# Building the S5 Toeplitz matrices from padded strips: full rows, one issuing queue, no zeroing

## The reference

```python
bu = jnp.einsum('blgn,gpn->blgp', uf.astype(jnp.complex64), b_bar)
a = jnp.broadcast_to(lam_bar, (1, seq, S5_GROUPS, S5_STATE))
_, states = lax.associative_scan(_linear_recurrence_combine, (a, bu), axis=1)
y = jnp.einsum('gnp,blgp->blgn', c, states).real + d.astype(f32) * uf
y = jax.nn.gelu(y.reshape(bsz, seq, D_MODEL))
y = y * jax.nn.sigmoid(y @ glu_w.astype(f32) + glu_b.astype(f32))
```

## Time and profile before

| | us |
|---|---|
| median of 3 runs | 1308.99 (1308.8 to 1311.32) |
| the profiled execution, its own time | 1309.56 |
| its span, first to last instruction | 1307.8 |
| PE busy | 1253.6 (96%) |
| DVE busy | 694.8 (53%) |
| ACT busy | 465.5 (36%) |
| POOL busy | 58.1 (4%) |

### The profile page before, as it was taken

One profiled execution on the slowest core, in us unless ns is written; L12 is line 12 of the kernel. 1 busy time (PEld: TensorE's weight loads), 2 busy tenths in 40 slices (PEclk: granted clock), 3 DMA queues, 4 the chain that ended last, 5 costly groups with the idle time before them and its releaser, 6 DMA issues.

```text
span 1307.8 us, 16043 instructions
## 1 busy us (share of the span) xinstructions
PE 1253.6 (96%) x6253; PEld 1039.9 (80%) x6253; DVE 694.8 (53%) x822; ACT 465.5 (36%) x481; POOL 58.1 (4%) x64
## 2 busy tenths in 40 slices
PE   2779999999999999999999999999999999999997
PEld 2768778888887888888888888888788888887886
DVE  8797874444444445555556464554355454444433
ACT  4834544242423333324223332332233232323222
POOL 2960000000000000000000000000000000000000
PEclk9989999999999999999999999999999999999999
DMA  5053323333322323322313223233332323222231
GB/s 112 2 136 100 96 88 105 96 96 96 96 86 81 96 88 114 103 100 96 105 33 121 79 65 103 65 96 96 97 97 88 104 90 102 90 72 89 88 101 73
DMA packets 147791, 119.18 MB, mean 91 GB/s; under 512 B 12857, under 2 KB 140017, under 8 KB 147761
## 3 DMA queue, kind: packets, MB, share of 16 engines
q1 hardware_dynamic: 143584, 115.78, 28.5%
q10 hardware_dynamic: 4176, 2.98, 1.1%
HBM read 114.29 MB, written 2.10 MB: 89 GB/s over the span
## 4 chain that ended last, share of the span: by engine, by line
PE 89%; DVE 4%; ACT 3%; issue 1%; DMA 1%; ACTq 1%; SPq 0%; DVEq 0%
PE bank L673 25%; PE bank L675 25%; PE bank L674 25%; PE bank L769 2%; PE bank L770 2%; PE bank L771 2%; PE bank L780 1%; ACTq L398 1%; DVE w_lo L1126 1%; PE bank L797 1%; PE bank L795 1%; PE bank L796 1%; DVE tmp L1116 1%; DMA w_raw<-in_s_glu_w_dram 1%; PE bank L625 1%
## 5 line engine op out<-in xcount | busy, mean ns | idle before, releaser
L673 PE MATMUL bank<-u_hi,w_hi 128*128 128x512 f32 x960 | 375.5, 391 | 2.0 <-DVE xT L1390 1.1
L675 PE MATMUL bank<-u_hi,w_lo 128*128 128x512 f32 x960 | 374.0, 390 | 0.0
L674 PE MATMUL bank<-u_lo,w_hi 128*128 128x512 f32 x960 | 373.8, 389 | 0.0
L1126 DVE TENSOR_TENSOR w_lo<-w_raw,w_hi 128x2048 fp32r<-128x2048 f32 x112 | 256.7, 2292 | 200.2 <-ACT w_hi L850 199.8
L850 ACT ACTIVATE w_hi<-w_raw 128x2048 fp32r<-128x2048 f32 x112 | 213.5, 1906 | 188.6 <-PE bank L675 146.4
L673 PEld LDWEIGHTS bank<-u_hi,w_hi 128*128 128x128 f32 x960 | 180.3, 188 | 40.5 <-issue 2.0
L675 PEld LDWEIGHTS bank<-u_hi,w_lo 128*128 128x128 f32 x960 | 180.3, 188 | 37.6
L674 PEld LDWEIGHTS bank<-u_lo,w_hi 128*128 128x128 f32 x960 | 180.3, 188 | 37.4 <-issue 0.5
L673 PE MATMUL bank<-h_hi,w_hi 128*128 128x512 f32 x352 | 137.3, 390 | 2.8 <-DVE w_lo L1126 2.8
L674 PE MATMUL bank<-h_lo,w_hi 128*128 128x512 f32 x352 | 137.1, 389 | 0.0
L675 PE MATMUL bank<-h_hi,w_lo 128*128 128x512 f32 x352 | 137.0, 389 | 0.0
(11 more groups left out here) (199 smaller groups left out, 1352.2 us busy)
## 6 DMA issues: line engine op xcount, KB each, us to landing
w_raw<-in_ret_w_qkvg_dram SPq DMA_DIRECT2D x24, 1024.0 KB, 5.0
w_raw<-in_ffn_w_gate_dram SPq DMA_DIRECT2D x22, 1024.0 KB, 5.1
w_raw<-in_ffn_w_up_dram SPq DMA_DIRECT2D x22, 1024.0 KB, 5.1
w_raw<-in_ffn_w_down_dram SPq DMA_DIRECT2D x32, 704.0 KB, 4.2
w_raw<-in_ret_w_o_dram SPq DMA_DIRECT2D x8, 1024.0 KB, 5.1
w_raw<-in_s_glu_w_dram SPq DMA_DIRECT2D x4, 1024.0 KB, 6.0
s<-in_x_dram ACTq DMA_DIRECT2D x2, 1024.0 KB, 12.2
s_w<-in_x_dram SPq DMA_DIRECT2D x1, 2048.0 KB, 10.0
```

The lines of the kernel that those rows point to most:

```text
L673: pe.matmul(o, w_hi[w][:, w_cols], hi, start=first, stop=False)
L674: pe.matmul(o, w_hi[w][:, w_cols], lo, start=False, stop=False)
L675: return pe.matmul(o, w_lo[w][:, w_cols], hi, start=False, stop=end)
L1126: dve.tensor_tensor(w_lo[s][:, :], w_raw[:, s, :], w_hi[s][:, :].bitcast(F32), ALU.subtract).then_inc(w_lo_ready[s], 1)
```

## The change

Each strip now carries its own zeros. Four pairs j lie interleaved (element m of pair i at 4 m + i), behind `LEAD` = 448 zeros, so that a row of four matrices shifted by 16 r columns is one run of 512 floats that starts 64 r floats earlier. One DMA moves, for one r, one half and eight pairs, 16 full rows of 2 x 512 floats (64 KB), zeros included; `toep` is no longer zeroed by ACT. Instead POOL zeroes the leading parts of the strips once at the start (64 partitions x 1792). `toeplitz(queue, part)` issues the 16 DMAs of a part, and SP issues all four parts: part 0 ahead of the x load, parts 1 and 2 behind it, part 3 behind the first GLU load. `strip_out` writes with a stride of four floats, and `y_inputs` reads `toep` with that stride. Strip 1 moves up between the tables of the last input stage (c = 3), strip 4 ahead of the transposes of x; `y_inputs` 0 to 3 no longer wait for `seg_done` 2 (0 and 1 wait for their part only, 2 and 3 for `seg_done` 1), strip 6 comes ahead of that wait and `keep_clock` behind it. ACT issues no Toeplitz DMA any more; it runs a small Gelu right behind strip 6 and splits the first GLU weights between gelu 3 and 4 instead of ahead of gelu 0.

```diff
     if _c == 2:
-        S5_FILLS += [("strip", 0)]
+    if _c >= 2:
+        S5_FILLS += [("strip", _c - 2)]
...
-S5_FILLS += [("b", 6), ("b", 7), ("strip", 1), ("strip", 7), ("strip", 2), ("strip", 3)]
+S5_FILLS += [("b", 6), ("b", 7), ("strip", 2), ("strip", 7), ("strip", 3)]
+Y_BANK = [6, 7, 2, 3, 0, 1, 4, 5]
...
-    _place(_fill, SHARED + _n % 4)
+    _place(_fill, SHARED + _n % 2)
 for _kind in ("y", "yt"):
     for _k in range(8):
-        _place((_kind, _k), _k)
+        _place((_kind, _k), Y_BANK[_k])
...
+LEAD = (STEPS - 1) * N * JB
+GROUP = LEAD + P * JB
...
-        toep = r_1[:, :].rearrange("p (g m) -> p g m", g=G)
+        toep = r_1[:, :].rearrange("p (h k m) -> p h k m", h=2, k=NBLK)
-        strip = w_raw[0:2 * N, :, :].rearrange("p s a -> p (s a)").rearrange("p (j m) -> p j m", j=J)
+        strip = w_raw[0:4 * N, :, 0:2 * GROUP].rearrange("p s (k m) -> p s k m", k=2)
...
-        def toeplitz_half(queue, part, half):
-            queue.wait_ge(toep_zeroed, 2 * part + 2)
+        def toeplitz(queue, part):
             for k in (2 * part, 2 * part + 1):
                 b, fill = S5_AT[("strip", k)]
                 queue.wait_ge(bank_free[b], fill + 1)
-            js = slice(PART * part, PART * part + PART)
-            gs = slice(J * half + js.start, J * half + js.stop)
-            for r in range(STEPS):
-                queue.dma_start(toep[N * r:N * r + N, gs, N * r:P],
-                                strip[N * half:N * half + N, js, 0:P - N * r]).then_inc(toep_loaded[part], 16)
+            for half in range(2):
+                row = 2 * N * (part // 2) + N * half
+                for r in range(STEPS):
+                    at = LEAD - N * JB * r
+                    queue.dma_start(toep[N * r:N * r + N, half, 2 * part:2 * part + 2, :],
+                                    strip[row:row + N, part % 2, :, at:at + P * JB]).then_inc(toep_loaded[part], 16)
...
+            sp.wait_ge(pads_zeroed, 1)
+            toeplitz(sp, 0)
             b, fill = S5_AT[("tb", 4 * NTAB - 1)]
             sp.wait_ge(bank_full[b], fill + 1)
             sp.wait_ge(tb_ready, 2 * NTAB)
             sp.wait_ge(tc_last_ready, 1)
             sp.dma_start(x_tok, x[0].rearrange("(t p) d -> p t d", p=P)).then_inc(x_loaded, 16)
-            toeplitz_half(sp, 0, 0)
-            toeplitz_half(sp, 0, 1)
-            toeplitz_half(sp, 1, 0)
-            toeplitz_half(sp, 2, 0)
-            for part in range(2):
+            toeplitz(sp, 1)
+            toeplitz(sp, 2)
+            for part in (0, 2):
                 sp.wait_ge(toep_loaded[part], 16 * 2 * STEPS)
             load_unit(0, 0, glu_v[:, :, 0:256], KT, 256)
-            toeplitz_half(sp, 3, 0)
-            for part in range(2, 4):
+            toeplitz(sp, 3)
+            for part in (1, 3):
...
-            strips(1)
+            strips(2)
             strips(NBLK - 1)
-            strips(2)
             strips(3)
+            strips(4)
...
-            strips(4)
             strips(5)
...
-                    pe.matmul(o, u[:, jj, half, :], toep[:, J * half + jj, :], start=(jj % 4 == 0), stop=False)
+                    pe.matmul(o, u[:, jj, half, :], toep[:, half, jj // JB, jj % JB::JB],
+                              start=(jj % 4 == 0), stop=False)
+            pe.wait_ge(toep_loaded[0], 16 * 2 * STEPS)
+            y_inputs(0)
+            y_inputs(1)
+            pe.wait_ge(seg_done, 1)
+            pe.wait_ge(toep_loaded[1], 16 * 2 * STEPS)
+            y_inputs(2)
+            y_inputs(3)
+            strips(6)
             pe.wait_ge(seg_done, 2)
-            for k in range(4):
-                if k % 2 == 0:
-                    pe.wait_ge(toep_loaded[k // 2], 16 * 2 * STEPS)
-                y_inputs(k)
-            strips(6)
+            keep_clock(s5_open("y", 6)[0], 8)
             pe.wait_ge(toep_loaded[2], 16 * 2 * STEPS)
             y_inputs(4)
             y_inputs(5)
-            keep_clock(s5_open("y", 6)[0], 8)
             for k in range(4):
                 y_states(k)
             pe.wait_ge(toep_loaded[3], 16 * 2 * STEPS)
...
-            toeplitz_half(act, 1, 1)
...
-            toeplitz_half(act, 2, 1)
             strip_out(6)
-            split_weights(0, 0)
-            toeplitz_half(act, 3, 1)
+            act.activation(small[:, 25:26], eps[:, :], ACT.Gelu_apprx_tanh)
...
                 gelu(k)
+                if k == 3:
+                    split_weights(0, 0)
...
             pool.memset(fb[:, :, :, :], 0.0).then_inc(fb_zeroed, 1)
+            pool.memset(strip[:, :, :, 0:LEAD], 0.0).then_inc(pads_zeroed, 1)
```

More of the change, by code:

```diff
@@ L332, in trunk @@
         tc_ready = sem("tc_ready")
-        toep_zeroed = sem("toep_zeroed")
+        pads_zeroed = sem("pads_zeroed")
         diag_ready = sem("diag_ready")
@@ L575, in strips @@
                 ps, full = s5_open("strip", k)
+                o = ps[2 * N * (k // 4):2 * N * (k // 4) + 2 * N, :]
                 for i in range(JB):
                     for ri in range(2):
[L578 removed]
+                        pe.matmul(o[:, P * i:P * i + P], fb[:, ri, JB * k + i, :],
                                   r_tc[:, ri, JB * k + i, :, :], start=(i == 0 and ri == 0), stop=False)
                 for i in range(JB):
[L581 removed]
+                    mm = pe.matmul(o[:, P * i:P * i + N], ident[0:2 * N, 0:2 * N], d_diag[:, JB * k + i, :],
                                    start=False, stop=(i == JB - 1))
@@ L594, in _ @@
                     pe.wait_ge(diag_ready, 1)
-                    strips(0)
+                if c >= 2:
+                    strips(c - 2)
                 s5_tables(c, 1)
@@ L903, in s5_input_out @@
                      ps[:, :].rearrange("p (j r c) -> p j r c", j=JB, r=2)).then_inc(free, 1)
-            def zero_toeplitz(k):
-                g = PART * (k // 2) + J * (k % 2)
-                act.activation(toep[:, g:g + PART, :].rearrange("p g m -> p (g m)"),
-                               eps[:, :].broadcast_to([P, 8 * P]), ACT.Copy, scale=0.0).then_inc(toep_zeroed, 1)
             def s5_steps_out(k):
@@ L916, in strip_out @@
                 ps, free = s5_full("strip", k)
-                copy(strip[:, JB * k:JB * k + JB, :].rearrange("p j m -> p (j m)"), ps[0:2 * N, :]).then_inc(free, 1)
+                rows32 = slice(2 * N * (k // 4), 2 * N * (k // 4) + 2 * N)
+                copy(strip[rows32, k % 4 // 2, k % 2, LEAD:GROUP].rearrange("p (m i) -> p i m", i=JB),
+                     ps[rows32, :].rearrange("p (i m) -> p i m", i=JB)).then_inc(free, 1)
             s5_table_out(0, 0)
@@ L925, in _ @@
                 s5_input_out(2 * c - 2)
-                if c == 2:
-                    strip_out(0)
-                if c == NTAB - 1:
-                    zero_toeplitz(2)
+                if c >= 2:
+                    strip_out(c - 2)
                 s5_table_out(c, 1)
                 s5_input_out(2 * c - 1)
-                if c < NTAB - 1:
-                    zero_toeplitz(c - 1)
-                else:
-                    act.wait_ge(tb_ready, 2 * NTAB)
-                    for ri in range(2):
-                        copy(ct_last[:, ri, :, :], ct[:, ri, J - JB:J, :]).then_inc(ct_copied, 1)
+            act.wait_ge(tb_ready, 2 * NTAB)
+            for ri in range(2):
+                copy(ct_last[:, ri, :, :], ct[:, ri, J - JB:J, :]).then_inc(ct_copied, 1)
             s5_input_out(NBLK - 2)
             s5_input_out(NBLK - 1)
-            strip_out(1)
-            zero_toeplitz(3)
+            strip_out(2)
             strip_out(7)
-            for k in range(4, 8):
-                zero_toeplitz(k)
-            strip_out(2)
             strip_out(3)
-            toeplitz_half(act, 1, 1)
+            strip_out(4)
             for k in range(KT):
@@ L950, in _ @@
                 copy(xT[:, k, :], ps[:, :]).then_inc(free, 1)
-            strip_out(4)
             strip_out(5)
-            toeplitz_half(act, 2, 1)
             strip_out(6)
-            split_weights(0, 0)
-            toeplitz_half(act, 3, 1)
+            act.activation(small[:, 25:26], eps[:, :], ACT.Gelu_apprx_tanh)
             def gelu(k):
```

1 line of the change is left out of this document (removed).

## The result

| | before | after |
|---|---|---|
| median of the runs beside each other, us | 1309.35 (1308.8 to 1311.32) | 1320.21 (1319.99 to 1320.78) |
| ratio, 95% interval | | 1.0079, 1.0065 to 1.0092 |
| the profiled execution, its own time | 1309.56 | 1320.78 |
| its span | 1307.8 | 1318.9 |

A forecast was written before the change was run, and what follows sets the result against it. It took part 3 of toep, landed at 110.1, as the bound; SP's single line would bring it at 114.4, 4.3 us later, rounded to 3.6: 1309.56 + 3.6 = 1313.2 profiled, median 1312.6, range 1304 to 1316.5.

The forecast's parts named there:

- the fast rival: SP's queue: long runs issue like DRAM loads, at 0.46 us; part 3 lands 4.0 us earlier, 1305.0; chance 0.2.
- Steps 1 and 2: Strip 1 on PE ends at 58.25, its strided copy takes 0.6 (bounds 0.6 and 1.1); SP starts part 0 at 58.95.
- Step 3: SP's queue: part 0 takes 9.9 us, to 68.9; x, issued then, lands 10.0 later, at 78.9.
- Step 5: Strip 5 on PE takes 2.2, to 87.6, and is out of PSUM at 88.3, 1.3 us earlier than before.
- Step 7: SP's queue: GLU load 0.6, part 3 9.9 plus 0.7 for a stretched issue, to 111.6; landing 2.8 later, 114.4.
- a rival of 8%: PE's y_inputs: the 16 B strided read halves the pace, 2.0 us more, 1314.6; chance 0.08.
- The other banks of y only let `y_inputs` 0 to 3 start early; nothing: PE's y products: new banks allow an earlier start only in a stretch that isn't the bound; cost nothing.
- The clock: Rival: PE idles 4.5 us for part 3, its clock falls for 7 us, 3.5 more, 1316; chance 0.1.
- The rounding from 4.3 down to 3.6: Part 3's delay on PE's path, cut because errors of steps 2 to 5 were thought to lean lower.

The follow-up runs named there:

- e9: Kernel before with strips 4 to 6 and keep_clock moved ahead, SP issuing all of part 1, ACT its halves of parts 2 and 3 back to back: 1309.73 us, ratio 1.0004.
- e12: e9 unchanged, run again for ten more runs and a second profile, against the kernel before: 1309.71 us, ratio 1.0.
- e4: Changed kernel plus 14 idle products behind y_states 3, ahead of the wait for part 3, to keep the clock: 1320.65 us, ratio 1.0084 to the kernel before.
- e5: Changed kernel with the x load issued ahead of part 0 on SP, as before the change: 1320.51 us, ratio 1.0076 to the kernel before.
- e1: Changed kernel with ACT again issuing the second halves of parts 1 to 3 (two queues): 1318.45 us, ratio 1.007 to the kernel before.
- e7: As e1, but each DMA moves only the columns right of its shift (output not the reference's): 1316.57 us, ratio 1.0046 to the kernel before.
- e8: Changed kernel with two issuing queues, unit stride and y in banks 0 to 7 in order, together: 1311.93 us, ratio 1.0018 to the kernel before.
- e14: e8 with SP issuing the first GLU load behind its half of part 3, not ahead: 1309.43 us, ratio 1.0 to the kernel before.
- e3: Changed kernel with y in banks 0 to 7 in order and y_inputs 0 to 3 again behind seg_done 2: 1319.23 us, ratio 1.0078 to the kernel before.
- e2: Changed kernel without interleaving: each matrix has its own 112 zeros, strip_out and y_inputs at unit stride: 1319.68 us, ratio 1.0079 to the kernel before.
- e10: Kernel before with each Toeplitz DMA moving full, unshifted rows of 64 KB (output not the reference's): 1316.26 us, ratio 1.0049.
- e13: e9 with SP issuing the first GLU load only when part 2 has landed: 1306.99 us, ratio 0.998 to the kernel before.
- e11: e9 with 14 idle products added ahead of strip 6 to keep the clock: 1313.8 us, ratio 1.0025 to the kernel before.

## Why the prediction was right in sign and wrong in size

**What held.** The GLU's start is what moves, and it comes out one for one at the end. The bound is the arrival of part 3 through SP's line. The issue of a full row costs what a short one did: 0.635 from start to start against the 0.62 taken; the fast rival (0.46) is dead. Part 2 took 12.3 us from its first issue to its landing against 12.1, the transposes of x 6.46 against 6.5. PE waited 3.56 us for part 3, where 4.5 was forecast; that these are close is luck, since part 3 came 3.3 us later than forecast and `y_states` 3 ended 4.3 later (114.16, not 109.9).

**The steps that failed**, in the order of the sum:

- *Steps 1 and 2, +1.7.* SP starts on part 0 at 60.66, not 58.95. 0.5 is `strip_out`, which with its 16-byte stride takes the upper bound, 1.11, not the lower that was chosen. The other 1.2 lie in the stretch before; it differs by 1.0 between two executions of one kernel as well (x issued at 66.78 in e9, at 65.80 in e12), so no cause in the change is shown for it.
- *Step 3, +1.4 and -1.3.* Part 0 has an issue of 1.42 us; x lands 8.7 us after its issue, not 10.0 (why was not tried). They cancel.
- *Step 5, +0.5.* The copy of strip 5 takes 1.08, again the stride.
- *Step 7, +2.0 and -1.1.* Two issues of 1.83 us instead of one small stretch of 0.7: part 3 was done issuing at 116.0, not 111.6. It landed 1.7 us later, not 2.8: the load had been through at 109.48, ahead of the last issues.
- *`y_inputs` at a stride, taken as 0: +1.9.* The bound of +1.97 was the right end. It was called a rival of 8% and kept out of the sum on the ground that a strided stationary load costs PE nothing; but that is the other operand, and no row spoke of the moving one.
- *"The other banks of y only let `y_inputs` 0 to 3 start early; nothing": +1.1.* Looked at for what it releases early, not for who opens banks 0 and 1 next. That is the GLU, at the end of the stretch.
- *The clock: +0.5.* The rival was right that it falls (PE idle 3.56), but it put 3.5 us on it. Only the transposes lost; the strided `y_inputs` take 3.83 at full clock (e4) and 3.90 at half (e5).
- *The rounding from 4.3 down to 3.6: -0.7*, in the wrong direction. The errors leaned the other way, because each unknown had been taken near its low end.

Sum: 3.6 forecast, and 1.7 + 0.1 + 0.5 + 0.2 (part 2) + 0.9 + 1.9 + 1.1 + 0.5 + 0.7 = 7.6 from these points, 11.2 in all by these rounded terms; measured 11.05 at the GLU's start. The range was too narrow for two reasons. Costs with the same sign were each put at their low end and their high ends never added: part 3 at 114.4 + 0.5 + 0.5 (the two copies) is 5.3 us late, and with 1.9 for the stride that is 7.2, or 1316.2, already at the end of the range (1316.5) without any stretched issue beyond the 0.7. The 3.9 us beyond that were put at nothing or not foreseen: 1.2 in the stretch ahead of strip 1, 1.1 for the banks, 0.9 for the stretched issues of part 3 less its quicker landing, 0.5 for the clock, 0.2 for part 2.

**What the experiments add.** The cause is not one thing. The line of issues sets the time in the changed kernel (e5, where an earlier x wins nothing). Behind it, level with each other, lie the transfers of part 3 and PE's own chain with the stride (e1: 115.57 and 115.4); e7 takes the first away and is held by the second. With both eased (e8), the load ahead of part 3 is what is left (e14). The wait for banks stands by itself at the end (e3). The Trainium skill (SBUF — State Buffer, Door 1: The DMA port swizzle) says that an access which crosses into another 16-byte line pays; what e2 measures agrees, for both engines, at a stride of exactly 16 B: 7.46 against 3.71 us for 64 records on PE, 1.11 against 0.59 for a copy on ACT. The Trainium skill's rule to coalesce small transfers (DMA: Bandwidth & Descriptors, Rules for kernel authors) gets no support from filling rows up to 64 KB: the issue gets no cheaper (0.59 us), and the bigger transfer costs (e10, +6.5 us). Fewer transfers, which is what the rule asks for, were not tried: there were 64 in every run.

**Still open.** What stretches single issues of SP to 1.4 to 2.6 us. The stretched issues near 64, 104 and 113 us of the changed kernel fall together with transfers of instructions; that is a coincidence in time and nothing more was tried. Nor was it tried to read `toep` at other strides. In e13 the chain of waits goes through the landing of the GLU load (105.24) and ACT's split of it, so the next gain there would not be in `toep`; this was not tried.

## What to carry to other kernels

Count the issues in a queue before the bytes, but then ask whether the bytes fit behind them: 64 DMAs at 0.64 us in one line were the bound here, and spread over two queues, the transfers with the load ahead of them were, and PE's own slower products. Never take a stride of 16 B on PE's moving operand or a copy's output as free when no row shows it; it about doubled both. And when a big load starts from one queue while another still issues small transfers that somebody waits for, put a wait between them: a few tenths of a us in the order decided over some 7 us, and the wait made a kernel with two groups of times (median 1309.7) into one that is always in the short one (1307.0).

## What the runs showed that was not expected

- An 8 KB DMA issued 0.27 us behind a 1 MB load on another queue took 8.39 us to land; 0.39 us ahead of it, 2.22 us (e12, e9). The order of two issues makes the two groups; the clock that falls in the wait adds some 2 us to the long one.
- `y_inputs` with the 16-byte stride takes 3.83 us for 32 records at the full clock (e4) and 3.90 at half (e5); without the stride 1.97 and 3.68 (e8, e2).
- A PE idle of 2.46 us was followed by a lower clock (strip 6 in e13 takes 3.07 us, in e11, without the idle, 1.94), and cost nothing since PE waited for a DMA afterwards. An idle of 2.70 us in e8 was not: the clock stood at 1.00 behind it. The length of the idle alone does not tell.
- Costs behind one another: undone alone 1.8, 0.5 and 1.0 us by the medians, together 8.3 (e1, e2, e3, e8).
